# The last two V projection items in three single passes on split weights and inputs

## Chip, cores and metric

The kernel runs on one core of one Trainium2 chip. The metric is the device time of one execution in microseconds (us). The granted clock of TensorE has two levels, 1.2 and 2.4 GHz; the profile writes them as 0.50 and 1.00.

## The reference

Two decoder layers over 256 tokens of width 1024, all float32. The first is an RWKV-7 time mixer with a dense SwiGLU, the second a state-space mixer with a top-2-of-8 expert SwiGLU. The change lies in the time mixer, and what matters of it is this:

```python
xx = token_shift(x) - x
xs = x[None] + xx[None] * mu[:, None, None, :]
r, k, v = jnp.einsum('sbtc,scd->sbtd', xs[:3], w_rkv)
...
kk = kk / jnp.maximum(jnp.linalg.norm(kk, axis=-1, keepdims=True), 1e-12)
k = k * (1.0 + (a - 1.0) * k_a)
y = wkv7_scan(rh, heads(decay), kh, vh, -kk, kk * ah)
...
bonus = jnp.sum(rh * kh * r_k, axis=-1, keepdims=True) * vh
```

v is a product of a 256 x 1024 input with a 1024 x 1024 matrix.

## The kernel before

Activations lie as [128 partitions, 8 chunks, 256 tokens]. The square weights come as 16 items of 1 MB (128 x 2048), four each for K, R, V and the output product; an item gives two chunks of 128 output columns. In the numbering of the kernel items 0 to 3 are K, 4 to 7 are R, 8 to 11 are V and 12 to 15 the output. They go through a ring of four buffers (RING) that SyncE (SP) fills in order of use: the load of item n is issued when the counter `used` has reached n - 3, and TensorE (PE) raises `used` by one as it ends an item.

An item is done in one of two ways. `project` (line 714) multiplies float32 weights by the float32 input, 16 matmuls of 256 columns, each of which stands in the trace as two records. `project_split` (line 720) does it in three single passes: ScalarE (ACT) writes the weights, rounded to fp32r, into RHI (`weight_high`, line 391, two halves), VectorE (DVE) subtracts them from the item and writes the rest into RLO, which lies over the ring buffer itself (`weight_low`, line 1459, two halves, each waits for its half of RHI), and PE multiplies high by high, low by high and high by low, 48 matmuls. RHI has two buffers, so `weight_high(n)` waits for the item before the last split one to be done. The inputs are split in the same way: XRH, XRL for R, and XVH, XVL for V. The tuple SPLIT (line 32) names the items done so: 4 to 9, numbered 0 to 5 within it. Items 10 and 11, the last two of V, are plain.

The engines run in parallel, each in its own order as written, and meet at semaphores. Around the change the orders are these:

- PE: `project_split(4)` and `(5)` (items 8, 9), then `head_sums` of T3 (line 780), which waits for the eight T3 products (`rk` at 8); then items 10 and 11 with `project` (line 711); then, once ACT has copied the last of V (`sq_out` at 12), for each of four groups `local_products(g)` (line 832, waits for `hat` at g + 1) and `by_token(g)` (16 transposes, lines 843 and 850). `by_token(0)` waits for `kk` at 8 first, since it writes the PSUM banks 4 to 7 in which the head sums lie. `local_products(g)` of the later groups waits for DVE's mask products (`m_sb`).
- ACT: decays, a copy of R, `weight_high(5)`, then four copies of V from PSUM to VV (`project_out(2, part, VV)`, line 381), each after its item. Later the copies of the transposed tiles (line 455).
- DVE: `weight_low(4)`, `weight_low(5)`, the eight T3 products (line 1508), the product AG by KK (line 1510), for four groups the "hat" products of keys, decays and receptances (lines 1519 to 1528), then four bonus products T3 by VV (line 1533), each of which waits for its copy of V and raises `kk`, the last to 8; then the mask products MB and MK (line 1543).
- GpSimd (POOL): two products DW (line 1982), after all hat products and item 11, then one mask product LT for each group (line 1993), after the transposes of the group.

The rest of the time mixer (a triangular solve in small matmuls), the output product from 245 us, the dense SwiGLU from 287 us, the state-space layer and the experts follow.

Of the kernel before, what the change touches and what calls it, by code (L numbers as in the profile page):

```python
# [28 lines left out]
NFFN = FF // P  # L29
NGLU = 8  # L30
NRING = 4
SPLIT = (4, 5, 6, 7, 8, 9)
ORDER = (4, 5, 6, 7, 0, 1, 2, 3, *range(8, 16))
NG = 4
STEP = 4
# [46 lines left out]
def build(nc, xT, prm_d, con_d, wsq, wffn, wglu, wmoe, lora1_d, lora2_d, s5p_d, s5b_d, s5c_d, rout_d, out_d):  # L82
    with ExitStack() as ctx:
# [3 lines left out]
        def at(name, shape, dt, off_kb=None, off=None):  # L87
            o = base + (int(off_kb * 1024) if off is None else off)
            n = int(np.prod(shape[1:])) * 4
            assert o + n <= usable, (name, o, n)  # L90
            return nc.alloc_sbuf_tensor_at(name, shape, dt, offset=o)
# [3 lines left out]
        def S(name):  # L95
            if name not in names:
                names[name] = ctx.enter_context(nc.semaphore(name))
            return names[name]
# [22 lines left out]
        VV = at("VV", [P, KC, T], F32, r(16))  # L121
# [10 lines left out]
        XV = at("XV", [P, KC, T], F32, r(105))  # L132
        XRH = at("XRH", [P, KC, T], F32R, r(64))
        XRL = at("XRL", [P, KC, T], F32R, r(72))
        XVH = at("XVH", [P, KC, T], F32R, r(88))
        XVL = at("XVL", [P, KC, T], F32R, r(96))
# [102 lines left out]
        def prm(name, j=None):  # L239
            o = PARAMS.index(name) * KC  # L240
            if j is None:
                return PRM[:, o:o + KC].unsqueeze(2).to_broadcast([P, KC, T])
            return PRM[:, o + j:o + j + 1]

        def half(bank, h):
            return PS[:, bank, h * T:(h + 1) * T]

        def flat(ap):
            return ap.rearrange("p a b -> p (a b)")

        def item(n):
            return RING[:, n % NRING, :], S(f"f_in{n % NRING}"), 16 * (n // NRING + 1)
# [107 lines left out]
        def _(act):  # L360
# [18 lines left out]
            def project_out(m, part, dest):  # L379
                act.wait_ge(S("used"), 4 * m + part + 1)  # L380
                act.activation(flat(dest[:, 2 * part:2 * part + 2, :]), PS[:, part % 2, :], ACT.Copy)\
                   .then_inc(S("sq_out"), 1)
# [8 lines left out]
            def weight_high(n):  # L391
                t = SPLIT[n]
                w, landed, value = item(t)
                act.wait_ge(landed, value)
                if n >= 2:
                    act.wait_ge(S("used"), SPLIT[n - 2] + 1)
                for h in range(2):
                    cols = slice(h * D, (h + 1) * D)
                    act.activation(RHI[:, n % 2, cols], w[:, cols], ACT.Copy).then_inc(S("w_hi"), 1)
# [44 lines left out]
                decays(g)  # L444
            project_out(1, 3, RR)
            weight_high(5)
            for part in range(4):
                project_out(2, part, VV)

            act.wait_ge(S("used"), 12)  # L450
            for g in range(NG):
# [237 lines left out]
        def _(pe):  # L689
# [18 lines left out]
            def products(outs, w, x):  # L708
                for h, out in enumerate(outs):
                    for k in range(KC):  # L710
                        mm = pe.matmul(out, w[:, h * D + k * P:h * D + (k + 1) * P], x[:, k, :], start=k == 0, stop=k == KC - 1)  # L711
                return mm

            def project(m, part, x):
                t = 4 * m + part
                w, landed, value = item(t)
                pe.wait_ge(landed, value)
                if t >= 2:
                    pe.wait_ge(S("sq_out"), t - 1)
                products((half(part % 2, 0), half(part % 2, 1)), w, x).then_inc(S("used"), 1)  # L720

            def project_split(n, xh, xl, input_at=None):
                t = SPLIT[n]
                if t >= 2:
                    pe.wait_ge(S("sq_out"), t - 1)
                for h in range(2):
                    pe.wait_ge(S("w_lo"), 2 * n + h + 1)
                    for k in range(KC):
                        if input_at is not None and h == 0 and k % 4 == 0:
                            pe.wait_ge(S("x_lo"), input_at + k // 4 + 1)  # L730
                        cols = slice(h * D + k * P, h * D + (k + 1) * P)
                        hi, lo = RHI[:, n % 2, cols], RLO[:, t % NRING, cols]
                        for m, (w, x) in enumerate(((hi, xh), (lo, xh), (hi, xl))):
                            mm = pe.matmul(half(t % 2, h), w, x[:, k, :], start=k == 0 and m == 0, stop=k == KC - 1 and m == 2)  # L734
                mm.then_inc(S("used"), 1)
# [42 lines left out]
            def head_sums(src, bank, done):  # L778
                for j in range(KC):
                    mm = pe.matmul(half(bank + j // 2, j % 2), head_ones, src[:, j, :], start=True, stop=True)  # L780
                mm.then_inc(S(done), 1)
# [28 lines left out]
            pe.wait_ge(S("rk"), 8)  # L810
            pe.wait_ge(S("kk"), 4)
            head_sums(T3, 4, "kk_ps")
            project(2, 2, XV)
            project(2, 3, XV)

            rows = (slice(0, CH), slice(CH, P))
            units = [(jj, c2, hh) for jj in range(2) for c2 in range(2) for hh in range(2)]
# [572 lines left out]
        def _(dve):  # L1390
# [68 lines left out]
            def weight_low(n):  # L1459
                t = SPLIT[n]  # L1460
                for h in range(2):
                    cols = slice(h * D, (h + 1) * D)
                    dve.wait_ge(S("w_hi"), 2 * n + h + 1)
                    tt(RLO[:, t % NRING, cols], RING[:, t % NRING, cols], RHI[:, n % 2, cols].bitcast(F32), ALU.subtract)\
                        .then_inc(S("w_lo"), 1)
# [38 lines left out]
            weight_low(4)  # L1504
            dve.wait_ge(S("sq_out"), 8)
            weight_low(5)
            for j in range(KC):
                stt(T3[:, j, :], RR[:, j, :], prm("r_k", j), KQ[:, j, :], ALU.mult, ALU.mult).then_inc(S("rk"), 1)
            dve.wait_ge(S("kk"), 4)
            link(tt(flat(AG[:, :, :]), flat(AG[:, :, :]), flat(KK[:, :, :]), ALU.mult))  # L1510
            dve.wait_ge(S("rk"), 8)
# [577 lines left out]
```

## Time and profile before

| | us |
|---|---|
| median of 3 runs | 1634.76 |
| lowest, highest | 1634.42, 1636.03 |
| the profiled execution | 1634.66 |
| its span in the trace | 1632.8 |
| PE busy | 1573.9 (96%) |
| DVE busy | 1271.3 (78%) |
| ACT busy | 958.1 (59%) |
| POOL busy | 87.8 (5%) |

The profile is that of one execution. Its page gives busy times, the chain of work that ended last (followed back from the end, at each step to what released it) and groups of instructions. A row of a timeline has the start in us, the duration, engine, line, operation, the tile written and those read, shapes, a count where rows are merged, and in brackets the idle time of the engine before it with what ended it. "issue" is a wait for nothing that the profile shows.

### The profile page before, as it was taken

The numbers are of one execution on the slowest core, as the hardware profiler recorded it, in microseconds if no ns is written. First come the engines' busy times: TensorE is split into PE (matmuls) and PEld (weight loads), VectorE is DVE, ScalarE is ACT, GpSimd is POOL, SyncE is SP. The second block draws the span as 40 slices with busy tenths as digits, with TensorE's granted clock in tenths as the row PEclk, the third lists the DMA queues.
The fourth block names the chain that finished last, engine by engine and source line by source line (L and its number), as shares of the span: only waits on it lengthen the run. The fifth ranks groups of instructions, "written<-read, shape, count | busy, mean of one in ns | idle before, by whom it ended". The sixth has DMA issues, their size and how long they took to land.

```text
span 1632.8 us, 28528 instructions
## 1 busy us (share of the span) xinstructions
PE 1573.9 (96%) x12396; PEld 1358.5 (83%) x12396; DVE 1271.3 (78%) x1432; ACT 958.1 (59%) x1056; POOL 87.8 (5%) x71
## 2 busy tenths in 40 slices
PE   8998788999999899999999999999999999999997
PEld 7888777999998787788888888888888888888885
DVE  6685442996866547988888898988888888898985
ACT  2733221667431137776777777776776776777673
POOL 0005102000003500000000000000000000000000
PEclk9999998999996999999999999999999999999999
DMA  7330002544425255799799799799799799799791
GB/s 293 110 136 4 4 2 104 181 171 178 159 87 208 77 209 232 294 390 369 288 401 369 290 400 371 298 391 386 282 391 401 267 391 396 272 391 400 276 381 67
DMA packets 72493, 421.19 MB, mean 258 GB/s; under 512 B 5024, under 2 KB 5152, under 8 KB 37424
## 3 DMA queue, kind: packets, MB, share of 16 engines
q1 hardware_dynamic: 72016, 418.26, 66.0%
q8 instruction: 98, 1.61, 0.4%
q0 software_dynamic: 352, 1.10, 0.2%
q14 instruction: 27, 0.22, 0.0%
HBM read 418.29 MB, written 1.05 MB: 257 GB/s over the span
## 4 chain that ended last, share of the span: by engine, by line
PE 92%; DVE 3%; POOL 2%; issue 2%; ACT 1%; DVEq 0%; POOLq 0%
PE PS L1286 37%; PE PS L1299 18%; PE PS L1099 12%; PE PS L1209 3%; PE PS L734 2%; PE PS L1084 2%; PE PS L1315 2%; PE PS L711 2%; PE PS L1292 1%; PE PS L888 1%; PE PS L755 1%; PE PS L905 1%; PE PS L1175 1%; PE PS L693 1%; DVE LOA L1796 1%
## 5 line engine op out<-in xcount | busy, mean ns | idle before, releaser
L1796 DVE TENSOR_TENSOR LOA<-EXA,WH 128x2048 fp32r<-128x2048 f32 x224 | 504.6, 2288 | 93.0 <-ACT WH L599 93.0
L599 ACT ACTIVATE WH<-EXA 128x2048 fp32r<-128x2048 f32 x224 | 416.9, 1909 | 4.8 <-DMA EXA<-in_wmoe 4.6
L1286 PE MATMUL PS<-WH,XGH 128*128 128x512 f32 x896 | 360.7, 403 | 0.0
L1286 PE MATMUL PS<-WH,XGL 128*128 128x512 f32 x896 | 350.6, 391 | 0.0
L1286 PE MATMUL PS<-LOA,XGH 128*128 128x512 f32 x896 | 349.9, 391 | 0.0
L1802 DVE TENSOR_TENSOR LOB<-EXB,WH 128x1024 fp32r<-128x1024 f32 x224 | 264.2, 1221 | 8.6 <-ACT WH L603 8.5
L603 ACT ACTIVATE WH<-EXB 128x1024 fp32r<-128x1024 f32 x224 | 224.1, 1052 | 0.0
L1286 PEld LDWEIGHTS PS<-WH,XGL 128*128 128x128 f32 x896 | 168.2, 188 | 35.7
L1286 PEld LDWEIGHTS PS<-WH,XGH 128*128 128x128 f32 x896 | 168.4, 188 | 33.4 <-DVE XGL L1894 1.8
L1286 PEld LDWEIGHTS PS<-LOA,XGH 128*128 128x128 f32 x896 | 168.8, 188 | 31.2
L1299 PE MATMUL PS<-WH,MHH 128*128 128x512 f32 x448 | 174.6, 390 | 3.8 <-DVE MHL L1890 3.8
L1299 PE MATMUL PS<-LOB,MHH 128*128 128x512 f32 x448 | 174.4, 389 | 0.0
L1299 PE MATMUL PS<-WH,MHL 128*128 128x512 f32 x448 | 174.3, 389 | 0.0
L638 ACT ACTIVATE MHH<-PS 128x256 fp32r<-128x256 f32 x112 | 43.1, 384 | 217.6 <-PE PS L1292 217.5
L1099 PE MATMUL PS<-FH,WHI 128*128 128x256 f32 x352 | 101.9, 289 | 5.8 <-DVE FL L1620 5.8
L1299 PEld LDWEIGHTS PS<-WH,MHH 128*128 128x128 f32 x448 | 84.1, 188 | 22.0 <-issue 4.8
L1099 PE MATMUL PS<-FL,WHI 128*128 128x256 f32 x352 | 100.8, 286 | 0.0
L1099 PE MATMUL PS<-FH,WLO 128*128 128x256 f32 x352 | 100.7, 286 | 0.0
L1299 PEld LDWEIGHTS PS<-WH,MHL 128*128 128x128 f32 x448 | 84.1, 188 | 17.5
L1299 PEld LDWEIGHTS PS<-LOB,MHH 128*128 128x128 f32 x448 | 84.1, 188 | 17.1
L1099 PEld LDWEIGHTS PS<-FH,WHI 128*128 128x128 f32 x352 | 68.6, 195 | 6.4 <-issue 6.4
L633 ACT ACTIVATE MSG<-PS 128x256 f32<-128x256 f32 x112 | 43.1, 384 | 51.1 <-PE PS L1286 51.1
(416 smaller groups left out, 2405.7 us busy)
## 6 DMA issues: line engine op xcount, KB each, us to landing
EXA<-in_wmoe SPq DMA_DIRECT2D x112, 2048.0 KB, 8.4
EXB<-in_wmoe SPq DMA_DIRECT2D x112, 1024.0 KB, 8.2
FRA<-in_wffn SPq DMA_DIRECT2D x22, 1024.0 KB, 6.0
RING<-in_wsq SPq DMA_DIRECT2D x16, 1024.0 KB, 4.9
FRB<-in_wffn SPq DMA_DIRECT2D x22, 512.0 KB, 3.8
GLUW<-in_wglu SPq DMA_DIRECT2D x8, 1024.0 KB, 13.0
LORA<-in_lora SPq DMA_DIRECT2D x1, 1536.0 KB, 18.6
CON<-in_con SPq DMA_DIRECT2D x1, 1156.0 KB, 20.4
```

The costliest lines, as they stand in the source:

```text
L599: act.activation(WH[:, n % 4, 0:NARROW], EXA[PAIR_SLOT[n // 2]][:, n % 2, :], ACT.Copy).then_inc(S("m_ahi"), 1)
L603: act.activation(WH[:, n % 4, NARROW:WIDE], EXB[PAIR_SLOT[n // 2]][:, n % 2, :], ACT.Copy).then_inc(S("m_bhi"), 1)
L633: act.activation(MSG[:, :, :], PS[:, p % 2, :].rearrange("p (e t) -> p e t", e=2)[:, :, 0:P], ACT.Silu)\
L638: act.activation(flat(MHH[:, :, :]), PS[:, 4, 0:2 * P], ACT.Copy).then_inc(S("m_hh"), 1)
L711: mm = pe.matmul(out, w[:, h * D + k * P:h * D + (k + 1) * P], x[:, k, :], start=k == 0, stop=k == KC - 1)
L734: mm = pe.matmul(half(t % 2, h), w, x[:, k, :], start=k == 0 and m == 0, stop=k == KC - 1 and m == 2)
L1099: mm = pe.matmul(out, a, b, start=start and k == 0 and n == 0, stop=stop and k == k_count - 1 and n == 2, skip_group_check=True)
L1209: mm = pe.matmul(half(4 + t % 4, h), GLUW[:, t, h * D + k * P:h * D + (k + 1) * P], HN[:, k, :], start=first and h == 0 and k == chunks[0] ...
L1286: mm = pe.matmul(PS[:, p % 2, :], x[:, k, :], w, start=k == 0 and m == 0, stop=k == KC - 1 and m == 2)
L1299: mm = pe.matmul(PS[:, 2 + c, :], x[:, e, :], w, start=start and m == 0, stop=stop and m == 2, skip_group_check=True)
L1796: tt(LOA[slot][:, n % 2, :], EXA[slot][:, n % 2, :], WH[:, n % 4, 0:NARROW].bitcast(F32), ALU.subtract)\
L1802: tt(LOB[slot][:, n % 2, :], EXB[slot][:, n % 2, :], WH[:, n % 4, NARROW:WIDE].bitcast(F32), ALU.subtract)\
```

## The change

SPLIT also names items 10 and 11. ACT makes their high parts, each behind a copy of V. DVE makes their low parts, that of item 10 ahead of the T3 products and that of item 11 behind them. PE does the two items with `project_split` on XVH and XVL.

```diff
-SPLIT = (4, 5, 6, 7, 8, 9)
+SPLIT = (4, 5, 6, 7, 8, 9, 10, 11)
...
             weight_high(5)
-            for part in range(4):
-                project_out(2, part, VV)
+            project_out(2, 0, VV)
+            weight_high(6)
+            project_out(2, 1, VV)
+            weight_high(7)
+            project_out(2, 2, VV)
+            project_out(2, 3, VV)
...
             head_sums(T3, 4, "kk_ps")
-            project(2, 2, XV)
-            project(2, 3, XV)
+            project_split(6, XVH, XVL)
+            project_split(7, XVH, XVL)
...
             weight_low(5)
+            weight_low(6)
             for j in range(KC):
                 stt(T3[:, j, :], RR[:, j, :], prm("r_k", j), KQ[:, j, :], ALU.mult, ALU.mult).then_inc(S("rk"), 1)
+            weight_low(7)
             dve.wait_ge(S("kk"), 4)
```

## Rows read from the trace of the kernel before

**Rows 1.** The page, part 4: chain that ended last, by engine.

```profile
PE 92%; DVE 3%; POOL 2%; issue 2%; ACT 1%; DVEq 0%; POOLq 0%
```

**Rows 2.** Chain of work, 78 to 124 us: start us, us, what.

```profile
86.59 11.74 PE PS L734 x96
98.33 3.46 PE PS L780 x16
101.79 13.83 PE PS L711 x64
...
116.29 1.98 PE PS L832 x64
118.27 1.46 PE PS L843 x12
```

**Rows 3.** Timeline of ACT from 87.5 us: start, us, line, operation, idle before.

```profile
87.40 0.58 ACT L381 ACTIVATE RR<-PS 128x512 f32<-128x512 f32 x1
87.88 1.99 ACT L399 ACTIVATE RHI<-RING 128x1024 fp32r<-128x1024 f32 x2
92.61 0.60 ACT L381 ACTIVATE VV<-PS 128x512 f32<-128x512 f32 x1 [2.74 <-PE PS L734]
98.37 0.60 ACT L381 ACTIVATE VV<-PS 128x512 f32<-128x512 f32 x1 [5.16 <-PE PS L734]
```

**Rows 4.** Timeline of DVE, 89 to 98 us.

```profile
89.03 2.36 DVE L1464 TENSOR_TENSOR RLO<-RING,RHI 128x1024 fp32r<-128x1024 f32 x2 [1.40 <-ACT RHI L399]
91.31 3.25 DVE L1508 SCALAR_TENSOR_TENSOR T<-RR,PRM,KQ 128x256 f32<-128x256 f32 x8
94.48 2.28 DVE L1510 TENSOR_TENSOR AG<-AG,KK 128x2048 f32<-128x2048 f32 x1
```

**Rows 5.** Timeline of DVE, 111 to 122 us.

```profile
112.59 1.88 DVE L1533 TENSOR_TENSOR T<-PS,VV 128x512 f32<-128x512 f32 x3
116.27 0.69 DVE L1533 TENSOR_TENSOR T<-PS,VV 128x512 f32<-128x512 f32 x1 [1.80 <-ACT VV L381]
...
121.27 1.29 DVE L1543 TENSOR_TENSOR MB<-PS,CON 128x512 f32<-128x512 f32 x2 [1.25 <-PE PS L832]
```

**Rows 6.** Ring loads: timeline of SP, 60 to 91 us; the page, part 6.

```profile
63.62 21.97 SPq L299 DMA_DIRECT2D RING<-in_wsq  x4
...
RING<-in_wsq SPq DMA_DIRECT2D x16, 1024.0 KB, 4.9
```

**Rows 7.** Timeline of POOL, 100 to 126 us.

```profile
115.78 2.08 POOL L1982 TENSOR_TENSOR DW<-CON,WC 128x512 f32<-128x512 f32 x2 [115.35 <-PE PS L711]
120.31 1.27 POOL L1993 TENSOR_TENSOR LT<-MB,CON 128x512 f32<-128x512 f32 x1 [2.45 <-PE PS L850]
124.12 1.27 POOL L1993 TENSOR_TENSOR LT<-MB,CON 128x512 f32<-128x512 f32 x1 [2.53 <-PE PS L850]
```

**Rows 8.** Stretches of us: length, busy us of PE, PEld, DVE, ACT, POOL, granted clock, DMA.

```profile
9.37:14.24 4.87, 0.00 (x0) 0.03 (x1) 4.19 (x6) 2.02 (x5) 0.00 (x0) 0.85 1.01 426
14.24:19.60 5.36, 5.36 (x13) 4.28 (x14) 5.21 (x10) 0.00 (x0) 0.00 (x0) 0.50 1.03 438
98.50:130.00 31.50, 30.81 (x388) 27.23 (x387) 25.11 (x49) 7.86 (x15) 5.89 (x5) 1.00 0.29 101
245.62:251.70 6.08, 6.08 (x14) 4.85 (x15) 3.72 (x6) 0.00 (x0) 1.94 (x4) 0.50 0.05 11
251.70:262.60 10.90, 10.90 (x52) 9.60 (x51) 0.69 (x1) 0.63 (x1) 0.89 (x2) 1.00 0.32 96
280.78:286.56 5.78, 0.00 (x1) 0.03 (x1) 5.63 (x9) 3.57 (x5) 5.78 (x1) 0.64 0.00 0
286.56:292.66 6.10, 6.10 (x28) 6.06 (x29) 5.70 (x10) 4.62 (x6) 2.08 (x2) 0.50 0.14 21
497.61:525.13 27.52, 27.52 (x513) 27.40 (x513) 16.09 (x27) 0.00 (x0) 8.56 (x7) 0.50 0.55 228
```

**Rows 9.** Groups of PE instructions, 498 to 525 us: count, busy us, mean ns, idle before.

```profile
L1175 PE MATMUL PS<-HN,BBT 32*128 32x64 f32 x512 | 27.6, 401 | 3.4 <-DVE HN L1403 3.4
```

## The prediction

> **What bounds the kernel now.** I read the page's chain of work first: of the whole span 92% of the chain lies on TensorE (PE) and 3% on VectorE (DVE) [rows 1]. An average like that says little of the stretch that changes, so the next view is the chain between 78 and 124 us [rows 2]. The reader should see one unbroken line of PE work there: items 8 and 9 in split form from 86.59 (96 matmuls, 11.74 us), the head sums of T3 (3.46 us, 98.33), the two plain items 10 and 11 (64 records, 13.83 us, 101.79), one ScalarE (ACT) copy of V, then (116.29) the groups of local products and transposes. So PE sets the pace here. But the third view, DVE in order of time, shows how little the second engine has to spare: after the last weight low part it works from 91.31 without a gap to 114.47 and waits only 1.80 us for V before its last bonus product [rows 4, 5]. That product ends at 116.96, and by_token(0) on PE, which waits for it (kk at 8), starts at 118.27 [rows 2, 5]. The slack of DVE at this meeting point is therefore 1.3 us (118.27 minus 116.96), and this is the number the change has to be held against.
>
> **PE's own work.** A split item is 48 matmuls and takes 11.74/2 = 5.87 us [rows 2]; a plain one takes 13.83/2 = 6.92 us. Two items give 2.10 us back, on the bounding engine. The Trainium skill (FP8 and Floating Point Precision, TensorE Precision Notes) counts true FP32 as four passes, so three passes would save a quarter, about 3.5 us on two items by that rule; the rows show 15% and not 25%, and I go by the rows.
>
> **ACT.** weight_high(6) goes behind the first copy of V, which starts at 92.61. A copy is followed by the next operation after 0.48 us (87.40 to 87.88) [rows 3], so the high part starts at 93.09; 1.15 us later (87.88 to 89.03) DVE can begin the first half of the low part [rows 3, 4]. weight_high(7) goes behind the second copy (98.37), starts at 98.85 and lets DVE begin at 100.00. Each costs ACT some 1.9 us, and ACT sits idle 5.16 us before the second copy [rows 3], and longer before the third, which waits for item 10 on PE, so ACT hides both; if this cover were gone the copies of V would come 1.9 us later each. The semaphore waits inside them (used at 9 and at 10) are those that the copies ahead of them have already met, and nobody is held behind them. Their data are there: the ring loads of items 10 and 11 are issued by 78.6 and at 85.3, and a ring load lands in 4.9 us [rows 6].
>
> **DVE.** This is where the price is. weight_low(6) stands ahead of the eight T3 products. It can't start at 91.31, when the engine comes free, but only when ACT has written the high part, at 94.24: a new wait of 2.93 us, with T3, the AG product and all the hat products queued behind it. The two halves take 2.28 us (89.03 to 91.31) [rows 4], so T3 starts at 96.52, 5.21 us later than now, and ends 3.17 us later (91.31 to 94.48), at 99.69. weight_low(7) waits until 100.00 and ends at 102.28. The AG product then starts at 102.28 and not at 94.48: 7.80 us later. From there to the end of the last hat product DVE has no wait today (94.48 to 112.59) [rows 4, 5] and none appears, since decays and V come earlier. The hat products end at 120.39. The four bonus products T3 by V then follow with no wait, because V is complete: three of them took 1.88 us, so each adds 0.60 and the last ends at 120.39 + 3 x 0.60 + 0.69 = 122.88.
>
> **PE again, now as the one that waits.** The head sums start when T3 is done, at 99.75 and not at 98.33 (1.4 us idle), end at 103.2; two split items end at 114.95; the ACT copy and local_products(0) follow at 115.6 to 117.6, earlier than today's 118.27 by 0.7 us. What was gained up to here is worth nothing, for by_token(0) waits until 122.9. Against 118.27 this is 4.65 us. After that nothing absorbs it: the groups follow each other at PE's pace, 3.81 us apart (120.31 to 124.12, the masks that wait for their transposes [rows 7]), while DVE's four mask products and GpSimd's (POOL) mask product are much shorter. POOL's two DW products (2.08 us at 115.78) wait for the last hat and now start at 120.4; they end at 122.5, before the first mask of POOL, which stood at 120.31 behind the transposes and moves to about 125.0 with them [rows 7]. SP's two ring loads that wait for items 10 and 11 are issued within 1 us of their present places and serve matmuls after 245 us, so the queue costs nothing.
>
> **The clock.** The new idle stretch of PE runs from 117.6 to 122.9, 5.3 us. Today the granted clock is 1.00 (2.4 GHz) from 98.50 to 130.00 [rows 8]. The trace has comparable idle stretches: 4.87 us up to 14.24, 5.78 us up to 286.56, and 3.4 us up to 497.61 [rows 8, 9]. After each the clock was at 0.50 (1.2 GHz), for 5.36 us after the restart at 14.24, for 6.10 us after that at 286.56; also for 6.08 us after the one at 245.62 [rows 8]. In such a stretch a plain matmul record takes 6.08/14 = 434 ns against 10.90/52 = 210 ns at the full clock, so half of the low time is lost: 2.7 to 3.1 us. The groups that follow here are dense (a group's local products and transposes stand back to back on PE [rows 2], and DVE waits 1.25 us for PE before the next group's mask product at 121.27 [rows 5]), so I take the loss whole, 2.9 us. If the fall doesn't come it is 0; if it came late in the restart it could be 3.4. The Trainium skill states the same behaviour (TensorE: Matmul & The Clock Gate, What's actually happening): the throttled state is the default, and activity releases it. It speaks against this change; no term of the sum needs it.
>
> **Sum.** Profiled execution: 1634.66 us (span 1632.8), the median of the runs is 1634.76, 0.1 apart. 1634.66 + 4.65 + 2.9 = 1642.2 us. Against the median that is +0.46%.
>
> **Rivals.**
> 1. The shift alone, without loss of clock: 1634.66 + 4.65 = 1639.3. For it: no idle stretch of the trace sits in just this place, and the local products are unlike the matmuls at those restarts. Against: three idle stretches of 3.4 to 5.8 us all ended at the low clock. 13%.
> 2. The clock falls and is not released soon. The row after 497.61 shows 27.52 us at 0.50 with PE at work throughout [rows 8, 9]. It decides from the point where the low clock outlasts the four groups (some 13.3 us of PE work after 122.9): then these cost double, 1634.66 + 4.65 + 13.3 = 1652.6. Against: after the other three restarts the full clock was back within 6.10 us [rows 8]. 6%.
> 3. The other side: PE's saving decides. If DVE's chain were not in the way of by_token(0), the two shorter items alone count: 1634.66 - 2.10 = 1632.6, 0.13% less. It needs kk at 8 by 116.2, hence DVE work of 4.56 us (two low parts) to fit into the 1.80 us idle before its last bonus product and 1.3 us of slack; it doesn't fit even without any wait on ACT. 3%, of which 1% for a gain of over 0.2%, which no row supports.
> 4. Between: the low parts find their high parts ready earlier than I think, so that only 4.56 - 1.80 = 2.8 us push DVE: kk at 8 at 119.7, by_token(0) 1.5 us late, no fall of the clock: about 1636.2. The start of weight_high(6) is tied to item 8's end on PE, so I see no way to it. 6%.
> That the passes are not made as described is hardly a rival: the same functions run six items today.
>
> **How the numbers follow.** My forecast, shift and clock, has 72%. The range must hold 8 in 10: it reaches from rival 1 less 0.8 us of spread between runs (1638.5) to the forecast with the full 3.4 us of low clock and 1.5 us for the fact that the later falls of the clock (ahead of 245.62, 286.56 and 497.61) may be released earlier or later relative to the work, an estimate from the 5.36 to 6.10 us of the rows: 1644.2. A measurement of this kernel can tell about 0.2% (3.3 us) from no change. Slower by more than that: forecast, rivals 1 and 2, together 0.91; within: rival 4 and two thirds of rival 3, together 0.08; faster: 0.01.
>
> **What would show it.** In the profile of the changed kernel: matmuls of L734's kind 96 more and none plain on XV, together near 11.7 us; the T3 products at 96.5, the AG product at 102.3, the last bonus product's end at 122.9; PE idle about 5.3 us ahead of the first transposes of V; the granted clock at 0.50 for some microseconds after it. I would be wrong if PE's transposes wait for something other than the bonus products, if DVE reaches them before 120, or if the clock row stays at 1.00.

## The result and the profile after

| | kernel before | changed kernel |
|---|---|---|
| median, us (14 runs each) | 1635.12 | 1640.8 |
| lowest to highest, us | 1629.84 to 1637.84 | 1635.68 to 1644.69 |
| ratio, 95% interval | | 1.0037 [1.0027, 1.0047] |
| profiled execution, us | 1634.66 | 1643.26 |
| its span, us | 1632.8 | 1641.4 |

The changed kernel is slower by 0.37%, which is 6.0 us of 1635. The prediction was 1642.2 us with a range of 1638.5 to 1644.2.

The two profiled executions differ by more than the medians (8.6 us in span). 1.0 us of it lies ahead of everything that changed: the first matmul of item 8 starts at 87.60 and not at 86.59. To compare places in two profiles I take the times from that matmul on; "later" below means later than in the kernel before by this count.

The page of the changed kernel, first part. PE and its records have hardly grown, DVE has 4 instructions and 4.2 us more.

```profile
PE 1575.3 (96%) x12428; PEld 1360.8 (83%) x12428; DVE 1275.5 (78%) x1436; ACT 962.2 (59%) x1060; POOL 87.7 (5%) x71
```

The chain of work of the changed kernel, 78 to 140 us (start, us, what), answers to [rows 2].

```profile
87.60 11.75 PE PS L738 x96
...
99.87 1.06 ACT RHI L399
...
103.31 2.21 DVE AG L1516
...
121.43 2.41 DVE T L1539 x4
123.88 2.82 PE PS L847 x12
...
127.22 1.91 PE PS L836 x64
```

In the kernel before this was one line of PE work. Now the chain leaves PE after item 9, goes over ACT's second new high part (99.87) and stays on DVE from 100.95 to 123.8: the low part, the AG product, all hat products and the four bonus products. PE comes back only with by_token(0).

The timelines of DVE and then of ACT show the same, and answer to [rows 3 to 5].

```profile
90.04 2.36 DVE L1468 TENSOR_TENSOR RLO<-RING,RHI 128x1024 fp32r<-128x1024 f32 x2 [1.40 <-ACT RHI L399]
95.20 2.36 DVE L1468 TENSOR_TENSOR RLO<-RING,RHI 128x1024 fp32r<-128x1024 f32 x2 [2.80 <-ACT RHI L399]
97.47 3.25 DVE L1513 SCALAR_TENSOR_TENSOR T<-RR,PRM,KQ 128x256 f32<-128x256 f32 x8
100.95 2.36 DVE L1468 TENSOR_TENSOR RLO<-RING,RHI 128x1024 fp32r<-128x1024 f32 x2 [0.22 <-ACT RHI L399]
103.23 2.29 DVE L1516 TENSOR_TENSOR AG<-AG,KK 128x2048 f32<-128x2048 f32 x1
...
121.35 2.48 DVE L1539 TENSOR_TENSOR T<-PS,VV 128x512 f32<-128x512 f32 x4
```

```profile
93.62 0.60 ACT L381 ACTIVATE VV<-PS 128x512 f32<-128x512 f32 x1 [2.74 <-PE PS L738]
94.11 2.00 ACT L399 ACTIVATE RHI<-RING 128x1024 fp32r<-128x1024 f32 x2
...
99.87 2.00 ACT L399 ACTIVATE RHI<-RING 128x1024 fp32r<-128x1024 f32 x2
110.29 0.60 ACT L381 ACTIVATE VV<-PS 128x512 f32<-128x512 f32 x1 [8.42 <-PE PS L738]
116.04 0.60 ACT L381 ACTIVATE VV<-PS 128x512 f32<-128x512 f32 x1 [5.15 <-PE PS L738]
```

The reader should see two waits for RHI that were not there, 2.80 us before the low part of item 10 and 0.22 us before that of item 11, and two low parts of 2.3 us. T3 starts 97.47 - 90.04 = 7.43 us behind the start of weight_low(5), where it took 2.28 us before; AG comes 103.23 - 1.01 - 94.48 = 7.74 us later.

Next, PE's timeline and the granted clock around the idle stretch (columns as in [rows 8]).

```profile
117.62 1.05 PE L836 MATMUL PS<-AR,KQ 64*64 64x128 f32 x32
123.88 0.90 PE L847 MATMUL PS<-CON,VV 128*128 128x128 f32 x3 [5.21 <-DVE T L1539]
```

```profile
118.60:123.88 5.28, 0.07 (x4) 0.00 (x0) 5.25 (x10) 0.00 (x0) 2.08 (x2) 0.95 0.29 119
123.88:126.70 2.82, 2.82 (x13) 2.82 (x14) 2.34 (x4) 1.20 (x2) 0.00 (x0) 0.50 0.00 0
126.70:131.00 4.30, 4.30 (x89) 3.79 (x87) 2.48 (x4) 2.36 (x5) 1.28 (x1) 1.00 0.01 4
```

PE stands still for 5.21 us, released by DVE's bonus products, and the clock is at 0.50 for the 2.82 us after the restart, then at 1.00 again. The first group's transposes took 1.90 us before (118.27 to 120.17 in the chain) and take 3.34 us now (123.88 to 127.22 in the chain).

### The profile page after: what moved, and what is told of

It is laid out like the page before. It is cut to its first block, busy times and chain, and to the rows that moved or that the text cites. A ratio compares the mean times of both kernels' runs of the same rounds, so it can differ in the third digit from the quotient of the medians.

```text
span 1641.4 us, 28602 instructions
## 1 busy us (share of the span) xinstructions
PE 1575.3 (96%) x12428; PEld 1360.8 (83%) x12428; DVE 1275.5 (78%) x1436; ACT 962.2 (59%) x1060; POOL 87.7 (5%) x71
## 4 chain that ended last, share of the span: by engine, by line
PE 90%; DVE 4%; POOL 2%; issue 2%; ACT 1%; DMA 1%; DVEq 0%; POOLq 0%
PE PS L1290 36%; PE PS L1303 18%; PE PS L1103 12%; PE PS L1213 3%; PE PS L738 2%; PE PS L1319 2%; PE PS L1088 2%; PE PS L1296 1%; PE PS L892 1%; PE PS L759 1%; PE PS L909 1%; PE PS L697 1%; PE PS L1179 1%; PE PS L715 1%; DVE LOA L1802 1%
```

## Experiments

Theory 1, that of the prediction: DVE's new work and its wait for ACT's high parts hold by_token(0) back by 4.65 us, and the fall of the clock in the idle stretch adds to it. Theory 2: the work of the low parts is the price by itself and the waits are hidden. Besides these, two rivals on the clock: it is most of the price, or none of it.

The first row is the measurement above; the others were taken in three series, each beside the kernel before. "keys" is the start of the first small matmuls after the four groups (132.51 in the kernel before), "solve" the start of the first step of the triangular solve after them (143.70). Both are given as later (+) or earlier (-) than in the kernel before, from item 8 on; the last column says how long the granted clock stayed at 0.50 in one piece from the idle stretch on, idle time included.

| kernel | ratio [95%] | by_token(0) | keys | solve | clock at 0.50, us |
|---|---|---|---|---|---|
| changed kernel | 1.0037 [1.0027, 1.0047] | +4.67 | +6.05 | +4.95 | 3.4 |
| after_again | 1.0039 [1.0026, 1.0052] | +4.67 | +6.00 | +4.67 | 3.4 |
| after_third | 1.0037 [1.0024, 1.0051] | +4.68 | +7.46 | +6.31 | 6.8 |
| only11 | 1.0045 [1.0031, 1.0060] | +4.67 | +6.01 | +4.69 | 3.4 |
| pool_both | 1.0043 [1.0028, 1.0059] | +5.58 | +8.06 | +6.74 | 10.2 |
| reorder | 1.0028 [1.0019, 1.0037] | +1.47 | +4.31 | +2.99 | 6.8 |
| fill_pe | 1.0022 [1.0011, 1.0033] | +4.67 | +4.68 | +3.36 | 0 |
| fill_again | 1.0015 [1.0004, 1.0026] | +4.75 | +4.76 | +3.44 | 0 |
| dve_extra | 1.0012 [1.0001, 1.0024] | +1.33 | +1.34 | +1.78 | 0 |
| decouple_plain | 1.0001 [0.9989, 1.0012] | +0.01 | +0.01 | -0.83 | 0 |
| decouple | 0.9991 [0.9978, 1.0004] | -2.31 | -1.11 | -2.43 | 0 |
| decouple_again | 0.9986 [0.9975, 0.9996] | -2.30 | -1.10 | -2.00 | 0 |
| decouple_pool | 0.9972 [0.9960, 0.9984] | -2.31 | -1.30 | -2.44 | 0 |

**DVE's work without its waits.** The kernel before, plus 4.56 us of DVE work in the two places; what it computes is not used.

```diff
             weight_low(5)
+            tt(flat(XR[:, :, :]), flat(KQ[:, :, :]), flat(RR[:, :, :]), ALU.subtract)
             for j in range(KC):
                 stt(T3[:, j, :], ...)
+            tt(flat(XK[:, :, :]), flat(KQ[:, :, :]), flat(RR[:, :, :]), ALU.subtract)
```

> The kernel before, with two subtractions of 128x2048 added on DVE (results not used), one ahead of the T3 products and one behind them: DVE gets the work of the two low parts (4.56 us) without any wait for ACT. Theory 1 (the price is the work plus the wait for the high parts): the hat products end 4.56 us later, at 117.15, the last bonus product at 119.6, by_token(0) starts 1.4 us later than 118.27, the clock stays at 1.00: about 1636.5 us against 1635.1. Theory 2 (DVE's work alone is the price, the waits are hidden): by_token(0) 4.6 us later, about 1639.7.

Measured 1.0012 [1.0001, 1.0024], 2.0 us. Timelines of DVE, then of PE:

```profile
90.64 2.28 DVE L1507 TENSOR_TENSOR XR<-KQ,RR 128x2048 f32<-128x2048 f32 x1
...
96.01 2.28 DVE L1510 TENSOR_TENSOR XK<-KQ,RR 128x2048 f32<-128x2048 f32 x1
...
116.33 2.48 DVE L1535 TENSOR_TENSOR T<-PS,VV 128x512 f32<-128x512 f32 x4
```

```profile
118.86 0.66 PE L843 MATMUL PS<-CON,VV 128*128 128x128 f32 x4 [1.26 <-DVE T L1535]
```

The 4.56 us of work push by_token(0) by 1.33 us, close to the 1.4 reckoned for work that first fills the 1.80 us of idle and the 1.3 us of slack. So 3.3 of the 4.67 us in the changed kernel are not DVE's work but go with the wait for the high parts (2.80 + 0.22 us of it stand in the rows above; the last 0.3 us I did not trace), and theory 2 falls.

**The change for item 11 alone.**

```diff
-SPLIT = (4, 5, 6, 7, 8, 9, 10, 11)
+SPLIT = (4, 5, 6, 7, 8, 9, 11)
...
             project_out(2, 0, VV)
-            weight_high(6)
             project_out(2, 1, VV)
-            weight_high(7)
+            weight_high(6)
...
-            project_split(6, XVH, XVL)
-            project_split(7, XVH, XVL)
+            project(2, 2, XV)
+            project_split(6, XVH, XVL)
...
-            weight_low(6)
             for j in range(KC):
                 stt(T3[:, j, :], ...)
-            weight_low(7)
+            weight_low(6)
```

> The change for item 11 alone: item 10 stays plain, the high part of 11 is made behind the second copy of V, its low part behind the T3 products. Theory 1 (what holds DVE is the wait for the high part behind the second copy, which ends at 100.00 whether or not item 10 is split): AG starts at 102.3 and by_token(0) at 122.9, as late as with both items, PE is idle for 4.3 us and the clock falls in most executions: 1640 to 1641, ratio 1.0030 to 1.0037. Rival (each low part adds its own share): half of the change's loss, ratio 1.0018 or less.

Measured 1.0045 [1.0031, 1.0060], 7.4 us: not half of the loss but all of it, and somewhat above the 1.0037 that I gave as the upper end. DVE's timeline:

```profile
92.07 3.25 DVE L1511 SCALAR_TENSOR_TENSOR T<-RR,PRM,KQ 128x256 f32<-128x256 f32 x8
100.72 2.36 DVE L1467 TENSOR_TENSOR RLO<-RING,RHI 128x1024 fp32r<-128x1024 f32 x2 [5.40 <-ACT RHI L399]
```

DVE does its T3 products in time and then waits 5.40 us for one high part, which ACT can only make behind the second copy of V. by_token(0) comes 4.67 us later, to the hundredth as with both items. PE is idle for 5.76 us ahead of it and not for the 4.3 that I gave: T3 being in time, the head sums don't wait the 1.4 us that they wait in the changed kernel. The low part of item 10 costs the changed kernel nothing of its own; it lies inside the wait for item 11.

**The order of DVE.** The changed kernel, with weight_low(6) behind T3 and weight_low(7) behind the first group of hat products.

```diff
-            weight_low(6)
             for j in range(KC):
                 stt(T3[:, j, :], ...)
-            weight_low(7)
+            weight_low(6)
...
                 tt(tokens(WD), tokens(KQ), last, ALU.mult).then_inc(S("hat"), 1)
+                if g == 0:
+                    weight_low(7)
```

> The changed kernel, with weight_low(6) behind the T3 products and weight_low(7) behind the first group of hat products, so that DVE waits for neither high part. Theory 1: the last bonus product ends at 119.6, by_token(0) 1.4 us later than in the kernel before, and PE, 2.1 us ahead in its items, is idle for about 3.4 us ahead of it; with or without a short fall of the clock 1636.5 to 1638.0. Theory 2 (the work alone is the price): as the changed kernel, 1641.

Measured 1.0028 [1.0019, 1.0037], which is 4.6 us; the medians, 1638.06 beside 1633.94 for the kernel before, lie 4.1 us apart. The place is as expected: by_token(0) 1.47 us later, both waits gone. The time is higher than the 1.4 to 2.9 us that I gave. PE's row and the clock:

```profile
120.36 0.90 PE L847 MATMUL PS<-CON,VV 128*128 128x128 f32 x3 [3.71 <-DVE T L1540]
```

```profile
116.60:120.36 3.76, 0.05 (x5) 0.00 (x1) 3.74 (x7) 0.00 (x0) 2.07 (x2) 0.89 0.43 179
120.36:126.30 5.94, 5.94 (x60) 5.61 (x64) 2.61 (x5) 2.39 (x4) 1.27 (x1) 0.50 0.00 0
```

PE, earlier with its items and held at nearly the same place, is idle for 3.71 us, and the clock is at 0.50 for the next 5.94 us. The four groups end 4.31 us later and not 1.47: 2.84 us for the clock, twice what the changed kernel's own profile shows. An order that repairs DVE leaves PE the idle time.

**PE kept at work.** The changed kernel with local_products(0) done three times.

```diff
                 pe.wait_ge(S("hat"), g + 1)
+                if g == 0:
+                    local_products(g, False)
+                    local_products(g, False)
                 local_products(g)
```

(With False the function doesn't raise m_ps.)

> The changed kernel, with local_products(0) done three times (the same values written to the same PSUM banks), so that PE is at work until about 121.5 instead of 117.6 and idle for 1.4 us instead of 5.3. Theory 1 (shift 4.6 us by DVE, some 1.4 to 2.9 us by the clock): the clock stays at 1.00 through the groups, by_token(0) starts as late as in the changed kernel, the time is about 1639.7. Rival (the clock is most of the price): below 1638. Rival (the clock costs nothing, since the groups are hidden behind something else): 1641, as the changed kernel.

> 'fill_pe' once more, beside the changed kernel in one series: the difference between the two is what the fall of the clock costs. Theory 1: 1.4 to 2.9 us, so fill_again at 1.0022 to 1.0028 with the changed kernel at 1.0037. Rival (the idle stretch costs nothing beyond the shift): both the same.

> The changed kernel once more, in one series with 'fill_again': 1.0037 to 1.0039 by the two series before; granted clock at 0.50 for 3 to 7 us from about 122 us.

Measured 1.0022 and 1.0015, against 1.0037 for the changed kernel in the first measurement and in the last series. The second is below the 1.0022 to 1.0028 that I gave for it. Medians of the last series: 1639.06 and 1642.01, and each of the 6 executions of the changed kernel there took longer than any of the 11 of fill_again. PE's row at by_token(0) in fill_pe, the clock in fill_pe and the clock in after_third:

```profile
122.72 0.66 PE L848 MATMUL PS<-CON,VV 128*128 128x128 f32 x4
```

```profile
122.70:132.20 9.50, 9.50 (x178) 8.66 (x176) 7.33 (x12) 5.30 (x11) 2.54 (x2) 1.00 0.02 3
```

```profile
122.63:129.00 6.37, 6.37 (x78) 6.04 (x80) 3.05 (x6) 2.39 (x4) 1.27 (x1) 0.54 0.00 0
```

by_token(0) stays where DVE puts it (+4.67), the clock doesn't fall, and 2.95 us are won back in the medians although PE does some 3.5 us more work (four sets of 32 matmuls, 0.87 us apart in its timeline). That is the price of the fall by the times. In the profiles of the changed kernel the groups lose 1.38, 1.33 and 2.78 us (keys minus by_token(0) in the table), depending on whether the clock came back after 3.4 or 6.8 us. The rival that the clock costs nothing falls. The one that it is most of the price had named 1638 us beside 1635.1, a ratio of 1.0018: fill_pe lies above that and fill_again below, so by the times alone the clock is about half of the loss, within wide bounds. What speaks against "most" is the place: with the clock up, by_token(0) is still 4.7 us late.

**A third profile of the same code.**

> The changed kernel as it is, to stand in one series with the others: ratio 1.0037 as measured first. Its profile shows whether the granted clock falls in the idle stretch of this execution as well, and for how long it stays at 0.50: theory 1 expects a fall, of 3 to 7 us; the rival that the fall was chance expects 1.00 throughout.

Measured 1.0039 [1.0026, 1.0052]; the clock fell here too and was at 0.50 for 3.4 us, in all three profiles therefore.

**The low parts on POOL.** The changed kernel, with both new low parts taken from DVE and given to POOL, which has nothing to do before 115 us.

```diff
 (DVE)
-            weight_low(6)
...
-            weight_low(7)
 (POOL, ahead of its wait for the hat products)
+            pool.wait_ge(S("w_lo"), 12)
+            weight_low(6)
+            weight_low(7)
```

> The changed kernel, with both new low parts made by POOL, which is idle until 115 us, and DVE as in the kernel before. Theory 1: nothing is left of DVE's delay, PE keeps the 2.1 us of its shorter items, by_token(0) starts at about 116.2: 1633.0 us. Rival: POOL takes more than 2.6 us for a half of 128x1024 (its rows show 1.27 us for 128x512), so that item 10 or 11 waits, or it slows DVE down while both write: 1636 or more.

Measured 1.0043 [1.0028, 1.0059]: theory 1 gave 1633.0 us, the median is 1641.56. POOL's row, and those of DVE behind the AG product:

```profile
94.90 12.32 POOL L1987 TENSOR_TENSOR RLO<-RING,RHI 128x1024 fp32r<-128x1024 f32 x4 [94.47 <-ACT RHI L399]
```

```profile
97.35 2.24 DVE L1523 COPY WC<-WD 128x8 f32<-128x8 f32 x1
...
99.83 2.58 DVE L1527 TENSOR_TENSOR AR<-RR,WD 128x256 f32<-128x256 f32 x1
...
104.89 2.62 DVE L1527 TENSOR_TENSOR AR<-RR,WD 128x256 f32<-128x256 f32 x1
107.43 0.68 DVE L1528 TENSOR_TENSOR AG<-AG,CS 128x512 f32<-128x512 f32 x1
```

POOL was quick enough: its four halves are done at 107.2, and PE does not wait for them. But three of the first group's four small DVE products, 0.42 us elsewhere, take 2.58 to 2.62 us each while POOL is at work, just the time of one of POOL's halves (median 2.598 us), and a copy of 0.17 us takes 2.24. At 107.43, POOL having ended, they are at their old length. The first hat group lasts 12.6 us (97.35 to 109.96) in place of 3.95. It was the rival's second half: DVE is not slowed down a little, it is held for the whole of a POOL instruction. The Trainium skill says so (SBUF — State Buffer, Terms): VectorE and GpSimd share a pair of ports that one of them holds for a full instruction, and the other blocks. These rows agree.

**The wait of by_token(0) taken off DVE.** by_token(0) waits for the bonus products only since they read the head sums in PSUM banks 4 to 7, which it overwrites. This kernel is 'reorder' with one thing more: ACT, idle there, copies the sums to T3, and DVE's bonus products go behind the masks.

```diff
 (ACT, behind weight_high(7))
+            act.wait_ge(S("kk_ps"), 3)
+            for g in range(NG):
+                act.activation(flat(T3[:, 2 * g:2 * g + 2, :]), PS[:, 4 + g, :], ACT.Copy).then_inc(S("t3_sb"), 1)
 (PE)
-                    pe.wait_ge(S("kk"), 8)
+                    pe.wait_ge(S("t3_sb"), 4)
 (DVE, behind the masks of group g and no longer ahead of all)
+                tt(flat(T3[:, pair, :]), flat(T3[:, pair, :]), flat(VV[:, pair, :]), ALU.mult).then_inc(S("kk"), 1)
 (POOL, level 1: its LT lies over VV)
+                        pool.wait_ge(S("kk"), 8)
```

> The kernel 'reorder' (low parts behind T3 and behind the first hat group), and in addition ACT copies the head sums from PSUM to T3 as soon as PE has made them, by_token(0) waits for these copies and no longer for the bonus products, and DVE makes each bonus product behind the mask products of its group. Theory 1 (by_token(0)'s wait for DVE's last bonus product turned the saving into a loss): the hat products end at 117.2, PE is idle for less than 1 us there, local_products(1) starts at about 118.4 in place of 120.17, the clock stays at 1.00: 1.75 us below the kernel before, ratio 0.9989. Rival (DVE's work as a whole is the bound in the stretch, wherever the wait stands): no gain, ratio 1.001 or more.

> The kernel before (items 10 and 11 plain) with the same ACT copies and the bonus products behind the masks: a control for 'decouple'. Theory 1: PE sets the pace there already, so nothing moves: within 0.3 us of the kernel before, ratio 1.000, and the gain of 'decouple' belongs to the split items. Rival (the wait for the bonus products costs the kernel before something too): ratio 0.999 or less.

> 'decouple' once more, to stand beside the next three: ratio 0.9989 by theory 1, 0.9991 as measured.

Measured 0.9991 [0.9978, 1.0004] and 0.9986 [0.9975, 0.9996] with the split items, 1.0001 [0.9989, 1.0012] with the plain ones. Only the second of the three intervals leaves 1 out, barely; the places in the profiles are clearer. PE and DVE in 'decouple':

```profile
115.48 0.66 PE L850 MATMUL PS<-CON,VV 128*128 128x128 f32 x4
...
118.15 1.10 PE L839 MATMUL PS<-AR,AG 64*64 64x128 f32 x32 [0.70 <-DVE MB L1548]
```

```profile
119.12 1.68 DVE L1552 TENSOR_TENSOR T<-T,VV 128x512 f32<-128x512 f32 x1
120.72 1.27 DVE L1548 TENSOR_TENSOR MB<-PS,CON 128x512 f32<-128x512 f32 x2
...
123.12 1.11 DVE L1552 TENSOR_TENSOR T<-T,VV 128x512 f32<-128x512 f32 x1
```

by_token(0) comes 2.31 us earlier than before, the next group's local products (118.15) wait only 0.70 us for the masks, and the clock stays up. Of these 2.31 us, 1.1 are left where the small matmuls begin, and not 1.75: beside POOL's products a bonus product takes 1.68 or 1.11 us. Whether ACT's copies would do without the new order of the low parts was not run.

**POOL out of DVE's way.** The same, and POOL's mask product of a group waits for that group's bonus product (`pool.wait_ge(S("kk"), 5 + g)` at level 0).

> 'decouple', and POOL's first mask product of each group waits for the bonus product of that group, so that the two no longer run at the same time. In 'decouple' the bonus products took 1.1 to 1.7 us beside POOL's products and 0.6 us elsewhere. Theory (DVE is held while POOL's product runs): the bonus products behind the second and third masks take 0.7 us, the groups go back to PE's 3.81 us, and the small solve starts some 0.5 us earlier than in 'decouple': ratio to the kernel before 0.9986. Rival (the longer products come from reading T3 in SBUF and not in PSUM): they stay at 1.1 us or more and the time is that of 'decouple'.

Measured 0.9972 [0.9960, 0.9984], median 1632.22 beside 1636.43 for the kernel before and 1642.01 for the changed one. DVE's rows:

```profile
119.26 0.68 DVE L1552 TENSOR_TENSOR T<-T,VV 128x512 f32<-128x512 f32 x1
...
122.26 0.68 DVE L1552 TENSOR_TENSOR T<-T,VV 128x512 f32<-128x512 f32 x1
123.51 1.29 DVE L1548 TENSOR_TENSOR MB<-PS,CON 128x512 f32<-128x512 f32 x2 [0.57 <-PE PS L839]
...
125.91 0.68 DVE L1552 TENSOR_TENSOR T<-T,VV 128x512 f32<-128x512 f32 x1
```

Each bonus product takes 0.68 us, all read T3 in SBUF as before, and DVE waits for PE again (0.57 us before the third group's masks). That is the theory's mechanism and not the rival's. The place of the small matmuls moves by 0.2 us only (-1.11 to -1.30) and the solve by 0.01 (-2.43 to -2.44), where I had said 0.5. The places don't explain the lower ratio, and the two kernels' intervals overlap, so that it is no proof of a gain over 'decouple'. Against the kernel before this version is faster beyond its interval.

## Why the prediction was right, point by point

- **PE's own work.** Expected 2.10 us on two items. In 'decouple', where by_token(0) waits for nothing, it comes 2.31 us earlier. ACT's rows above show item 11 alone: 116.04 - 110.29 = 5.75 us between the copies of V. In the kernel before it was 115.64 - 108.73 = 6.91 us, so 1.16 us an item:

```profile
108.73 0.60 ACT L381 ACTIVATE VV<-PS 128x512 f32<-128x512 f32 x1 [9.77 <-PE PS L711]
115.64 0.60 ACT L381 ACTIVATE VV<-PS 128x512 f32<-128x512 f32 x1 [6.31 <-PE PS L711]
```

  The sum by rows was right within 0.2 us. The quarter by the Trainium skill's count of passes (FP8 and Floating Point Precision, TensorE Precision Notes), 3.5 us on both items, did not appear.
- **ACT.** Expected free. It was, in time of its own; weight_high(6) began 0.49 us behind the first copy (94.11 against 93.62) and DVE 1.09 us after it (95.20), where I had 0.48 and 1.15.
- **DVE.** Expected: T3 5.21 later, AG 7.80 later, last bonus product's end at 122.88. Measured 5.15, 7.74, and 123.83 - 1.01 = 122.82. The steps were right, but their reading was not complete: the text dwells on the wait of 2.93 us ahead of weight_low(6), while 'only11' shows that weight_low(7), tied to the second copy of V, fixes the place alone.
- **by_token(0).** Expected 4.65 later, measured 4.67. (The prediction's own 122.9 - 118.27 is 4.63; the difference changes nothing.)
- **The clock.** A fall was expected and found in all three profiles of the changed kernel and in 'only11', 'pool_both' and 'reorder', the experiments with 3.7 us or more of idle PE. The term was mis-sized: 2.9 us, against 1.38, 1.33 and 2.78 us in the profiles. I had taken the length of the low stretch from restarts after which it was 5.36 to 6.10 us; here it was 2.8 us of work in the changed kernel's profile, since the clock came down only at the end of the idle time (granted clock 0.95 over the idle stretch) and was up again after 2.82 us of work. In after_third the low stretch was 6.8 us and the loss 2.78, nearly the forecast's. From the times the fall costs (1.0038 - 1.0018) x 1635 = 3.3 us, with some 1.7 us of uncertainty, which doesn't tell 1.8 (the mean of the three profiles) from 2.9. The prediction's upper bound of 3.4 us is half of the 6.8 us that [rows 8] show at 0.50 around 14.24 (a clock of 0.85 over 4.87 us, then 5.36 us); no profile lost that much here.
- **"After that nothing absorbs it."** Wrong by 1.1 to 1.3 us. In the changed kernel's three profiles the stretch from keys to solve is shorter by that (columns "keys" and "solve" of the table). Start of both in the kernel before and in fill_pe, by the chain, which can put a start up to 0.2 us behind the timeline of which the table is made:

```profile
132.51 0.97 PE PS L859 x26
...
143.70 2.02 PE PS L888 x62
```

```profile
137.04 0.97 PE PS L864 x26
...
147.08 1.81 PE PS L893 x62
```

  This is 11.19 us against 10.04 us for the same matmuls. The four turns of the stretch last 2.67, 2.95, 2.97 and 2.60 us in the kernel before (the start of line 859's first matmuls in each turn: 132.51, 135.18, 138.13, 141.10) and 2.67, 2.46, 2.45 and 2.46 us in fill_pe (137.04, 139.71, 142.17, 144.62). 'dve_extra', with PE's very instructions of the kernel before, keeps the long stretch (+0.44), but 'decouple_plain', also with plain items and the same work on PE, is 0.84 us shorter, so the split items are not the reason. Nor is it code alone: 'decouple' and 'decouple_again', the same kernel, differ by 0.42 us. The second to fourth turns of the kernel before have a pause each that the chain puts down to no semaphore ("issue", ending at 136.22, 139.96 and 143.70); fill_pe has none in its four turns, but one of 1.31 us earlier, among its added matmuls (up to 121.63). What makes the pauses come and go stays open.
- **Rivals.** The third (PE's saving decides) and the fourth (only 2.8 us push DVE) were not the case here; 'dve_extra' is the fourth by design, and gave its 1.3 us. The second (a low clock that outlasts the groups) was not seen in any of the profiles in this place. The first (the shift alone, 1639.3) lies 1.5 us below the median of 1640.8 and the forecast 1.4 us above it, so the time alone doesn't choose between the two. The clock rows do, with the fall in three profiles of three, and so does the gap between fill_again and after_third. So the mechanism is the forecast's; that its number lies no farther off is not because errors cancelled: the clock term was too large in two profiles of three, and the 1.2 us that were made up after the groups had no term at all, both on the same side.

Sum of what was measured: 4.67 (DVE) + 1.8 (clock, mean of three profiles) - 1.2 (keys to solve) = 5.3 us at the solve; the times say 6.0 [4.4, 7.7].

## What to carry to other kernels

Before an engine is relieved, look for the next meeting point with the engine that gets the work, and write down the slack there: here 2.1 us were saved on PE, 4.6 us of work went to an engine with 3.1 us to spare, and the wait for its input cost 3.3 us more. A wait placed in an engine's queue costs all that stands behind it, so the step that needs the latest input goes last among those that nobody waits for. And if the meeting itself is only about a buffer, let an idle engine empty the buffer: then the saving arrives.

## What the runs showed of the hardware

- The granted clock can stay low while PE works. In the profile of 'dve_extra' it was at 0.50 for 17 us in the middle of the state products, with PE busy for 14.94 of 15.00 us; ahead of the fall PE was idle for no more than a microsecond or so (busy 0.30 us from 215 to 216). This execution took 1646.78 us where the median of its kernel is 1636.0.

```profile
210.00:215.00 5.00, 4.69 (x196) 4.35 (x191) 2.02 (x6) 1.20 (x2) 0.00 (x0) 1.00 0.01 3
215.00:216.00 1.00, 0.30 (x10) 0.30 (x12) 0.58 (x3) 0.00 (x0) 0.00 (x0) 1.00 0.00 0
...
218.00:233.00 15.00, 14.94 (x247) 13.55 (x243) 0.41 (x1) 0.60 (x1) 0.00 (x0) 0.50 0.01 2
...
234.00:235.00 1.00, 1.00 (x38) 0.96 (x34) 0.00 (x0) 0.00 (x0) 0.00 (x0) 1.00 0.00 0
```

  The kernel before has no such stretch in this place; it has 27.52 us at 0.50 with PE at work throughout, at 497.61 [rows 8]. Executions of the kernel before lie up to 9.5 us apart (1629.06 to 1638.56 in the series of 'dve_extra') and those of 'dve_extra' 13.2 us (1633.56 to 1646.78), and the place and length of the low stretches is one thing that differs between profiles of the same code: 3.4 us in two profiles of the changed kernel, 6.8 us in the third, in the same place.
- While POOL works on tensors in SBUF, DVE's products of two SBUF tensors wait until POOL's instruction ends: 0.42 us become 2.6 in 'pool_both', 0.68 become 1.1 to 1.7 in 'decouple'. An idle POOL was no free place for work beside a busy DVE here.
- Three single passes on split operands (48 matmuls) against float32 matmuls (16): 5.75 against 6.91 us for an item of 1 MB, 17% less and not a quarter.
